# Activation stage of a hybrid decoder layer: how its one-hots, gate tiles and gate stores are formed

## The reference

```python
q = (xb @ wq).reshape(PEER_BLOCK, PEER_HEADS, 2, PEER_HALF)
s = jnp.einsum('thpd,hpkd->thpk', q, subkeys).astype(jnp.float32)
s_top, i_top = lax.top_k(s, PEER_TOPK)
cand = s_top[:, :, 0, :, None] + s_top[:, :, 1, None, :]           # 256 pairs a head
g_s, g_i = lax.top_k(cand, PEER_TOPK)
e = jnp.take_along_axis(cand_idx, g_i, axis=-1)                    # expert = i * 128 + j
g = jax.nn.softmax(g_s, axis=-1)
act = jax.nn.gelu(jnp.einsum('thed,td->the', u[e], xb))
return jnp.einsum('the,thed->td', g * act, v[e])
```

## Time and profile before

| | |
|---|---|
| median of 3 runs | 2477.82 us (2477.76 to 2481.19) |
| the profiled execution | 2477.28 us, span 2475.5 us |
| PE busy | 2105.6 us, 85% |
| DVE busy | 1687.7 us, 68% |
| POOL busy | 929.6 us, 38% |
| ACT busy | 812.3 us, 33% |
| moved by DMA | 547.71 MB, 220 GB/s of HBM traffic over the span |
| u columns, PE line 2374 | 3072 matmuls |
| one-hots, PE line 2390 | 768 records, eight to a unit |

### The profile page before, as it was taken

One profiled execution on the slowest core, in us unless ns is written; L12 is line 12 of the kernel. 1 busy time (PEld: TensorE's weight loads), 2 busy tenths in 40 slices (PEclk: granted clock), 3 DMA queues, 4 the chain that ended last, 5 costly groups with the idle time before them and its releaser, 6 DMA issues. The chain is left out here.

```text
span 2475.5 us, 31968 instructions
## 1 busy us (share of the span) xinstructions
PE 2105.6 (85%) x10417; PEld 1698.3 (69%) x10417; DVE 1687.7 (68%) x3076; ACT 812.3 (33%) x1519; POOL 929.6 (38%) x727
## 2 busy tenths in 40 slices
PE   8998976678887867969888788888877899999997
PEld 7774763334334646858788788887777788888885
DVE  4562007867231134798999999998756899998988
ACT  1331012133101021123455455455454333333331
POOL 1000333222000000015666556666666556554550
PEclk9999997687989688989899889989988899999998
DMA  5323429765513102226677777777878999999993
GB/s 188 78 53 109 141 84 317 285 233 207 201 61 109 51 0 80 64 84 220 199 258 249 230 234 258 252 251 241 292 261 315 373 397 392 395 397 392 387 386 126
DMA packets 243183, 547.71 MB, mean 221 GB/s; under 512 B 21598, under 2 KB 125712, under 8 KB 241771
## 3 DMA queue, kind: packets, MB, share of 16 engines
q1 hardware_dynamic: 114538, 287.33, 33.7%
q0 software_dynamic: 60736, 208.40, 23.0%
q10 hardware_dynamic: 67776, 50.34, 6.3%
HBM read 485.51 MB, written 60.02 MB: 220 GB/s over the span
## 5 line engine op out<-in xcount | busy, mean ns | idle before, releaser
L2374 PE MATMUL psum<-hH,uH 128*128 128x384 f32 x1024 | 364.8, 356 | 58.9 <-PEq L1934 19.7
L2076 POOL DMA_INDIRECT u_gather<-in_u_rows,gather_ids x160 | 202.5, 1266 | 520.0 <-DVE gather_ids L1889 421.9
L2192 POOL TENSOR_TENSOR uL<-u_raw,uH 128x1024 fp32r<-128x1024 f32 x125 | 312.4, 2500 | 197.6 <-ACT uH L2206 196.2
L2374 PE MATMUL psum<-hL,uH 128*128 128x384 f32 x1024 | 354.6, 346 | 0.0
L2374 PE MATMUL psum<-hH,uL 128*128 128x384 f32 x1024 | 353.9, 346 | 0.0
L2482 POOL DMA_INDIRECT v_gather<-in_v_rows,idx_now x160 | 252.7, 1579 | 235.4 <-DVE y_sample L2567 139.1
L2270 DVE CUSTOM_DVE_ANT_0 u_prod<-u_gather,h 128x1024 f32<-128x1024 f32 x160 | 251.5, 1572 | 102.8 <-DMA u_gather<-in_u_rows,gather_ids 94.8
L2616 PE MATMUL psum<-vH,wH 128*128 128x512 f32 x768 | 301.7, 393 | 21.3 <-DVE wL L2560 21.3
L2616 PE MATMUL psum<-vH,wL 128*128 128x512 f32 x768 | 301.1, 392 | 0.0
L2616 PE MATMUL psum<-vL,wH 128*128 128x512 f32 x768 | 300.7, 392 | 0.0
L2374 PEld LDWEIGHTS psum<-hH,uH 128*128 128x128 f32 x1024 | 202.8, 198 | 63.9 <-issue 42.8
(11 more groups left out here) (482 smaller groups left out, 3518.8 us busy)
## 6 DMA issues: line engine op xcount, KB each, us to landing
u_raw<-in_uT SPq DMA_DIRECT2D x128, 512.0 KB, 4.5
S<-in_v_rows SPq DMA_DIRECT2D x64, 512.0 KB, 10.6
v_rest<-in_v_rows SPq DMA_DIRECT2D x64, 512.0 KB, 6.7
activation_table<-acts ACTq DMA_DIRECT2D x128, 192.0 KB, 4.3
gate_table<-Gtile ACTq DMA_DIRECT2D x12, 2048.0 KB, 15.6
S<-gate_table SPq DMA_DIRECT2D x16, 768.0 KB, 7.8
S<-activation_table SPq DMA_DIRECT2D x16, 768.0 KB, 11.4
G_rest<-gate_table SPq DMA_DIRECT2D x16, 768.0 KB, 7.4
```

What stands on the lines that cost most here:

```text
L2076: c.nc.gpsimd.indirect_dma_start(c.ug[:, k % RG], None, c.A["u_rows"].rearrange("j i d -> (j i) d"), bass.IndirectOffsetOnAxis(ap=c.ids[:, ...
L2192: nc.gpsimd.tensor_tensor(uL[:, n % RU], u[:, n % RAW], uH[:, n % RU].bitcast(F32), ALU.subtract).then_inc(u_split, 1)
L2374: ins = nc.tensor.matmul(bank[n % 2][:, 0:ND], w[:, n % RU, d], x[:, d], start=m == 0, stop=m == len(parts) - 1)
```

## The change

In `stage_activate` the two one-hot tiles become one, `hot[:, buffer, 0:8]`, with i in 0 to 3 and j in 4 to 7. DVE makes the first six in one operation. ACT makes the last two: |j - iota|, then Relu(gate - gate x distance), which is the gate where they are equal and 0 elsewhere; the other two j are scaled as before. So ACT runs six operations of 128 elements a unit. PE writes token t's tile to every fourth column of the bank, and the eviction then reads the bank in order. The unit's order on ACT is evict, then a quarter of a gate store, then gate. A finished block is stored as four transfers, one in each of the next four units. `acts` has three buffers. Pass 0 has eight dots instead of twelve, the last pass 52 instead of 48. In the expert stage the five sums of the first group come behind its products and first three splits; in other groups the order is as it was. The route buffer of the sample is smaller.

```diff
-STEP_DOTS = ((2, 1) * 4, (6, 5) * 4, (6,) * 8, (6,) * 8)
+STEP_DOTS = ((1,) * 8, (6, 5) * 4, (6,) * 8, (7, 6) * 4)
...
+RA = 3
+BY_DVE = UNIT // 2
+STORES = 4
...
                 def slots_in(p):
                     act.wait_ge(res_mm, p)
-                    nc.scalar.activation(slots[:],
-                                         bank[5][:, 0:3 * P].rearrange("p (q n) -> p q n", q=3),
+                    nc.scalar.activation(slot_g[:, 0], bank[5][:, 2 * P:3 * P], ACT.Copy)
+                    nc.scalar.activation(slot_g[:, 1], bank[5][:, 2 * P:3 * P], ACT.Copy, scale=-1.0)
+                    nc.scalar.activation(slot_ij[:].rearrange("p u q t -> p q u t"),
+                                         bank[5][:, 0:2 * P].rearrange("p (q u t) -> p q u t", q=2, t=UNIT),
                                          ACT.Copy).then_inc(slots_ready, 1)
...
-                    nc.scalar.activation(G[:, blk % 2, :, j * UNIT:(j + 1) * UNIT].rearrange("p j t -> p t j"),
-                                         bank[2 + n % RB].rearrange("p (t j) -> p t j", t=UNIT),
+                    nc.scalar.activation(G[:, blk % 2, :, j * UNIT:(j + 1) * UNIT],
+                                         bank[2 + n % RB].rearrange("p (j t) -> p j t", t=UNIT),
                                          ACT.Copy).then_inc(g_ev, 1)
...
+                def store(blk, i):
+                    if i == 0:
+                        act.wait_ge(g_ev, (blk + 1) * BUNIT)
+                    part = slice(i * (NG // STORES), (i + 1) * (NG // STORES))
+                    act.dma_start(A["gates"][part, :, blk * (GS * TB):(blk + 1) * (GS * TB)].rearrange("g p n -> p g n"),
+                                  G[:, blk % 2].rearrange("p (g j) t -> p g (j t)", j=GS)[:, part]
+                                  ).then_inc(G_stored[blk % 2], 16)
+
+                def gate(p, n):
+                    k, h = n % PUNIT, n % RH
+                    act.wait_ge(slots_ready, p)
+                    if n >= RH:
+                        act.wait_ge(g_mm, n - RH + 1)
+                    for q in range(BY_DVE, UNIT):
+                        ins = nc.scalar.activation(hot[:, h, UNIT + q], c.iota[:], ACT.Abs,
+                                                   bias=slot_ij[:, k, 1, q:q + 1], scale=-1.0)
+                    ins.then_inc(distance, 1)
+                    act.wait_ge(hot_ready, n + 1)
+                    for q in range(BY_DVE):
+                        nc.scalar.activation(hot[:, h, UNIT + q], hot[:, h, UNIT + q], ACT.Copy,
+                                             scale=slot_g[:, 0, k * UNIT + q:k * UNIT + q + 1])
+                    act.wait_ge(distance, n + 1)
+                    for q in range(BY_DVE, UNIT):
+                        m = k * UNIT + q
+                        ins = nc.scalar.activation(hot[:, h, UNIT + q], hot[:, h, UNIT + q], ACT.Relu,
+                                                   bias=slot_g[:, 0, m:m + 1], scale=slot_g[:, 1, m:m + 1])
+                    ins.then_inc(gated, 1)
...
                 def unit(p, st, i):
                     n = unit_of(p, st, i)
                     j = n % PUNIT
-                    act.wait_ge(slots_ready, p)
-                    for k in range(j + GATE_LEAD if j else 0, min(j + GATE_LEAD + 1, PUNIT)):
-                        act.wait_ge(hot_ready, n - j + k + 1)
-                        for q in range(UNIT):
-                            ins = nc.scalar.activation(hot_j[:, k % RH, q], hot_j[:, k % RH, q], ACT.Copy,
-                                                       scale=slots[:, 2, k * UNIT + q:k * UNIT + q + 1])
-                        ins.then_inc(gated, 1)
                     if n:
                         evict(n - 1)
+                    if n >= BUNIT and n % BUNIT < STORES:
+                        store(n // BUNIT - 1, n % BUNIT)
+                    for k in range(j + GATE_LEAD if j else 0, min(j + GATE_LEAD + 1, PUNIT)):
+                        gate(p, n - j + k)
+
+                def flush():
+                    evict(NUNIT - 1)
+                    for i in range(STORES):
+                        store(NTB - 1, i)
...
-                    for q, hot in enumerate((hot_i, hot_j)):
-                        ins = V.tensor_tensor(hot[:, n % RH], c.iota[:].unsqueeze(1).to_broadcast([P, UNIT, P]),
-                                              slots[:, q, j * UNIT:(j + 1) * UNIT].unsqueeze(2).to_broadcast([P, UNIT, P]),
-                                              ALU.is_equal)
-                    ins.then_inc(hot_ready, 1)
+                    made = UNIT + BY_DVE
+                    V.tensor_tensor(hot[:, n % RH, 0:made], c.iota[:].unsqueeze(1).to_broadcast([P, made, P]),
+                                    slot_ij[:, j].rearrange("p q t -> p (q t)")[:, 0:made].unsqueeze(2)
+                                    .to_broadcast([P, made, P]), ALU.is_equal).then_inc(hot_ready, 1)
...
-                        ins = nc.tensor.matmul(bank[2 + n % RB][:, q * P:(q + 1) * P], hot_i[:, n % RH, q],
-                                               hot_j[:, n % RH, q], start=True, stop=True)
+                        ins = nc.tensor.matmul(bank[2 + n % RB].rearrange("p (j t) -> p t j", t=UNIT)[:, q],
+                                               hot[:, n % RH, q], hot[:, n % RH, UNIT + q], start=True, stop=True)
...
+                    first = r is None and b == 0
+                    for j in range(GS):
+                        product(r, b, j)
+                        if j:
+                            split(r, b, j - 1)
+                        elif not first:
+                            split(r, b - 1, GS - 1)
+                        if j == 0:
+                            dve.wait_ge(w_taken, g + 1)
+                        if not first:
+                            add(r, b, j)
+                    for s in range(0 if first else GS, GR):
+                        add(r, b, s)
```

More of the change, by code:

```diff
@@ L1897, in __init__ @@
         self.v16, self.cand = sb("v16", [P, 2, TOPK]), sb("cand", [P, TOPK * TOPK])
-        self.first, self.second, self.sample = ((sb("i16_" + n, [P, BATCH, 2, TOPK], U32), sb("gi_" + n, [P, BATCH, TOPK], U32))
-                                                for n in ("first", "second", "sample"))
+        self.first, self.second, self.sample = ((sb("i16_" + n, [P, k, 2, TOPK], U32), sb("gi_" + n, [P, k, TOPK], U32))
+                                                for n, k in (("first", BATCH), ("second", BATCH), ("sample", 2)))
         self.ab, self.abf = sb("ab", [P, BATCH, 2, TOPK], U32), sb("abf", [P, BATCH, 2, TOPK])
@@ L2093, in stage_activate @@
         a = c.acts
-        slots, prod = sb("slots", [P, 3, P]), sb("u_prod", [P, D])
+        slot_ij, slot_g, prod = sb("slot_ij", [P, PUNIT, 2, UNIT]), sb("slot_gate", [P, 2, P]), sb("u_prod", [P, D])
         b = c.route
         gsum = sb("gsum", [P, PH])
-        hot_i, hot_j = (sb(n, [P, RH, UNIT, P]) for n in ("hot_i", "hot_j"))
+        hot = sb("hot", [P, RH, 2 * UNIT, P])
         G = sb("Gtile", [P, 2, NKEYS, TB])
@@ L2180, in _ @@
                 for i in range(2):
-                    sp.wait_ge(G_stored[i], 16 * (NTB // 2))
-                    sp.wait_ge(a_stored[i], 16 * (GS // 2))
+                    sp.wait_ge(G_stored[i], 16 * STORES * (NTB // 2))
+                for i in range(RA):
+                    sp.wait_ge(a_stored[i], 16 * len(range(i, GS, RA)))
                 sp.dma_start(c.G_group[0], A["gates"][0]).then_inc(c.G_in[0], 16)
@@ L2211, in columns @@
                     act.wait_ge(u_mm, n + 1)
-                    if n >= 2:
-                        act.wait_ge(a_stored[n % 2], 16 * (n // 2))
-                    nc.scalar.activation(a[:, n % 2], bank[n % 2][:, 0:ND], ACT.Gelu_apprx_tanh).then_inc(u_act, 1)
+                    if n >= RA:
+                        act.wait_ge(a_stored[n % RA], 16 * (n // RA))
+                    nc.scalar.activation(a[:, n % RA], bank[n % 2][:, 0:ND], ACT.Gelu_apprx_tanh).then_inc(u_act, 1)
                     act.wait_ge(u_act, n + 1)
-                    act.dma_start(A["acts"][n], a[:, n % 2]).then_inc(a_stored[n % 2], 16)
+                    act.dma_start(A["acts"][n], a[:, n % RA]).then_inc(a_stored[n % RA], 16)
                 def gates_out(p):
@@ L2449, in _ @@
                     sp.dma_start(v[j], A["v_rows"][j]).then_inc(v_in[j], 16)
-                for i in range(2):
-                    sp.wait_ge(c.a_stored[i], 16 * (NKEYS // 2))
+                for i in range(RA):
+                    sp.wait_ge(c.a_stored[i], 16 * len(range(i, NKEYS, RA)))
                 def body(r, b):
@@ L2573, in body @@
                                   ).then_inc(w_taken, 1)
-                    product(r, b, 0)
-                    if r is not None or b:
-                        split(r, b - 1, GS - 1)
-                    dve.wait_ge(w_taken, g + 1)
-                    add(r, b, 0)
-                    product(r, b, 1)
-                    split(r, b, 0)
```

(12 more changed lines are left out.)

13 lines of the change are left out of this document (4 added, 9 removed).

## The result

The changed kernel takes 2460.17 us (median, 2456.82 to 2462.97) against 2477.79 for the one before beside it: ratio 0.9927, 95% interval 0.9909 to 0.9944. Faster, but by 18 us where 93 were forecast, and outside the range. Its profiled execution has a span of 2458.0 us.

The account below looks back on a forecast made before the run. DVE and PE were taken to run neck and neck, with ACT's store stalls holding nearly all DVE slack. Stretches of 83, 214, 216 and 173 us make 686 against 773 (-87), experts -6: 2477.3 - 93 = 2384 us, range 2353 to 2442.

Parts of the forecast that it names:

- the stall term: Activation passes: removing ACT's store stalls gives DVE 4.5 us each, 13.5 us for three in a pass; PE 25 us.
- Pass 3: Last activation pass: falls from 196 us to PE's floor of 173 us, with DVE below 138 and ACT 147.
- Pass 0: Activation stage's first stretch: four dots fewer save DVE 7.7 us before the first routing, 91 us becoming 83.
- One-hot term: DVE in each pass: one merged one-hot operation saves 10.9 us, and less waiting for GpSimd's subtractions saves 4 us.
- ACT's cost: ACT's cycle per unit: 3.95 us becomes 4.98 with six gating operations and store issues, 4.6 after eviction's gain; PE's is 5.06.
- Rival A: Strided PSUM writes double the unit's 0.81 us of one-hot matmuls, giving back 54 us, 2438 us; chance 0.17.
- Rival B: Four quarter stores block ACT's queue as long as one whole, 10.2 us a block; about +30 us, 2414 us; chance 0.07.
- Rival C: Abs not in gelu's table, so each unit swaps ACT tables twice; cycle 7.5 us, total 2531 us; chance 0.04.
- Rival D: DVE's waiting for GpSimd halves, passes fall to PE's floors, 23 us less, 2361 us; chance 0.70 jointly with the forecast.
- Experts: Expert stage's start: first sums moved behind splits start PE 6.2 us sooner, at 1919.3, and this carries to the end.
- The tail: Activation stage from 1880 us: no change counted, since its last gate store still goes out at once.

Follow-up runs that it names:

- e1: Kernel before with only the gate stores changed: each block stored in four quarters over the next four units; 2478.26 us, ratio 1.0001.
- e6: e4 with each gate block stored as one whole 2 MB transfer instead of quarters; 2442.26 us, ratio 0.9848.
- e4: Changed kernel with four dots put back from the last pass to pass 0 (twelve there, 48 in pass 3); 2434.12 us, ratio 0.9817.
- e11: e4 with the last gate block's four quarter stores spread, one in each of the first four tail columns; 2430.8 us, ratio 0.9811.
- e3: Changed kernel with GpSimd's subtraction cut to 128 of 1024 elements, all waits kept; 2349.97 us, ratio 0.9491.
- e13b: e4 with the last pass's 48 dots in steps of seven and five instead of six; 2446.89 us, ratio 0.9868.
- e7: e4 with all eight one-hots of a unit in one DVE operation, none on ACT; 2456.43 us, ratio 0.9909.
- e12: e4 with gate tiles unbroken in PSUM as before the change, the eviction going across them; 2439.76 us, ratio 0.9842.
- e2: Kernel before with GpSimd's subtraction cut to 128 of 1024 elements, all waits kept; 2361.14 us, ratio 0.9526.
- e15b: e11 with the expert stage's first-group sums back in the order of the kernel before; 2432.97 us, ratio 0.9810.

## Why the prediction was wrong, step by step

**The step that failed is the stall term, 13.5 us in pass 1 and again in pass 2.** The prediction took 4.5 us of DVE's idle time in each stall as slack that it would fill with work once the stall is gone, at the same collision rate. Both halves were wrong. The size came from one window with 5.5 us of idle time; 40 us that lie in the same way round the other two stalls of that pass have 3.7 and 3.6 (before):

```profile
1294.00:1334.00 40.00, 33.49 (x193) 33.04 (x192) 36.26 (x68) 22.04 (x44) 26.63 (x16) 0.91 0.77 254
1354.00:1394.00 40.00, 33.55 (x201) 33.10 (x200) 36.45 (x65) 19.45 (x39) 26.37 (x16) 0.91 0.80 265
```

All of DVE's waits that the profile lists in that pass are for gathered rows:

```profile
DVE u_prod L2270 <- DMA u_gather<-in_u_rows,gather_ids: 12.5, 6, 2.9
```

Only one of them, of 2.2 us, lies inside a stall; three come some 10 us behind one. e1, with the stalls alone taken out, idles 7.7 and 7.1 us less in passes 1 and 2, not 13.5, and DVE's busy time rises by 5.2 and 7.0: it gained nothing. e6 put the stalls back into the new kernel and lost nothing in these two passes. And the kernel after, without stalls, still leaves DVE idle for 17.6 us of pass 1 and 13.8 of pass 2, by the same cuts, where before left 19.5 and 17.4: the slack was not the stalls' alone.

DVE is the bound there, and a quarter of its busy time is collisions. My account of the rise is this: while ACT stands still, GpSimd, which waits for ACT's uH, stands soon too, and DVE works that time off uncontended. The trace of before fits: GpSimd subtracts during 24% of its nine stalls in the passes and during 41% of the rest, and the dots begun in a stall take 1314 ns against 1595. Kind by kind against the means outside, the DVE operations begun in the nine stalls are 12.5 us shorter in all (an estimate from these means); e1's DVE is busy 11.4 us longer than before's over the three passes. That this is the whole coupling stays my reading; no run isolates it. In pass 3, where DVE has room, the stalls do cost PE: 14 us by e6 (e1: 6.5), under the 25 forecast for three, and the tail takes part of it back (4 us in e6, 6.8 in e1).

**Pass 3, forecast 173 (PE's floor).** The floor was near enough: 176 in e4, 174 in e11, 170 in e3. The kernel had 199, since "four dots move to the last pass, where DVE has 58 us to spare" counted busy time and not order. Two thirds of the 23 us come from having seven dots in a step, one third from the four dots more (e13b, after).

**Pass 0, forecast -7.7.** Nothing came that the spread of the kernels lets me see. DVE did lose 6.9 busy us there, but its first routing then waited 14.4 us for ACT's exponential where it had waited 4.1, and ACT stands behind PE and PE behind GpSimd's subtractions, whose queue waits for dots. Why it waited longer stays open; no run tried it. The waits of 1107 to 1198 us, after and then before:

```profile
POOL u_gather L2079 <- DVE dots L2301: 22.0, 3, 11.8
...
DVE gsum L2316 <- ACT res_first L2224: 14.4, 1, 14.4
```
```profile
DVE gsum L2285 <- ACT res_first L2220: 4.1, 1, 4.1
```

e4 and the other kernels with twelve dots say that the four dots were nearly free in pass 0.

**One-hot term, -10.9 and -4 a pass.** Right: the earlier trace rows and the groups after give 89.0 + 64.1 + 5.5 against 55.0 + 75.1 + 14.1, 14.4 us less in pass 1. The collisions did not go with the operations, they moved to the dots and the routing, as the prediction chose. Passes 1 and 2 are by 15 and 12 us shorter, most of it this term: DVE's busy time fell by 13.1 and 8.6 between the copies of the slots. e7 gives two of eight on ACT 17.6 us over three passes.

**ACT's cost.** 0.60 + six operations of which the Relu takes 480: the cycle stays under PE's, and ACT is busy 63% in pass 3 (forecast 60).

**Rival A, strided PSUM writes: refuted.** In the trace after a unit's eight records span 1.05 us as in the earlier trace rows, and e12, which takes the stride away, is not faster. The rule of the Trainium skill ("Advanced Engine Details and Errata", section "PSUM Cachelines"), that a non-contiguous pattern significantly slows matmuls, did not show for 128-column f32 matmuls whose results lie 16 bytes apart:

```profile
1330.11 1.05 PE L2420 MATMUL psum<-hot 128*128 128x128 f32 x8
```

**Rival B, the stall splits: not in the passes**, where every store of an activation takes 0.34 to 0.36 us; but four quarters in one row do hold ACT (14.26 us). Its price had a slip: it gives ACT 159 us in pass 3 where the sum has 147 (32 x 4.6), and with 147 it is 15 us, not 30. **Rival C, table swaps: refuted**, the stage's gelu line has six loads, as before:

```profile
L2218 ACT ACT_TABLE_LOAD x6 | 7.7, 1283 | 0.1
```

**Rival D, collisions halve: no.** e2 shows what lay there: with the long subtraction gone, 4.7% or some 117 us.

**Experts, -6.2.** The start came as forecast: 1902.64 is 7.6 us behind the last dot's start, before 14.0. It is given back. The time from the last dot to the span's end is 561.4 to 564.0 us in the four kernels with the old order (before, e1, e2, e15b) and 559.3 to 564.0 in the others. The trace says where: after 200 matmuls of the stage PE is 62.5 us behind the last dot's start in the kernel after and 62.3 in the one before, and from there both keep one pace. Two waits for a low part lie between that before does not have, and with the second PE's granted clock falls (0.77 over the stretch shown):

```profile
1918.00 0.50 PE L2644 MATMUL psum<-vH,wH 128*128 128x512 f32 x1 [1.17 <-DVE wL L2590]
...
1937.89 0.80 PE L2644 MATMUL psum<-vH,wH 128*128 128x512 f32 x1 [3.26 <-DVE wL L2590]
```
```profile
1930.00:1945.00 15.00, 11.74 (x40) 9.19 (x39) 10.69 (x14) 4.60 (x6) 5.36 (x5) 0.77 1.03 406
```

The first is the fourth weight. The prediction had it ready 11.6 us behind PE's start; it came after 15.3, since three of the five sums ahead of it waited for gathered rows (0.47, 0.63 and 1.27 us), which the prediction put at nothing. The second is the eighth. Its low part stands behind DVE's first product of the third group, and that waits for its activation tile, here after and then before:

```profile
1935.68 0.56 DVE L2579 TENSOR_TENSOR wf<-S 128x384 f32<-128x384 f32 x1 [3.06 <-DMA S<-activation_table]
```
```profile
1954.45 0.56 DVE L2549 TENSOR_TENSOR wf<-S 128x384 f32<-128x384 f32 x1 [2.19 <-DMA S<-activation_table]
```

Counted from the last dot it comes 40.7 us behind it after and 42.9 before: 2.2 us sooner, where PE began 6.4 sooner. So at that place PE waits for what the transfers bring. DMA's share of 1.03 in that stretch points at the transfers' rate; no run took transfers away, so this last step stays argued.

**The tail, forecast 0.** It is 6 us longer by the earlier trace rows's cut. The step took the last gate store as going out at once, but it goes as four. From the last eviction to the last dot, with eight dots in the tail, the kernels with whole stores have 31.3 and 31.2 us (before, e6; e2, without collisions, 23.7), those with four quarters in one row 34.5 to 38.4 (e3 33.3), e1 among them with 38.1, and those with the quarters spread 33.4 to 35.0. So the growth goes with splitting the stores, and ACT's hold of 14 us is at most a part of it (under 1 us by e11 against e4). By what way the rest comes is open.

**The sum.** By the cuts of the earlier trace rows the forecast lost 8 us in pass 0, 36 in passes 1 and 2 (27 of them the stall term), 21 in pass 3, 6 in the tail and 5 in the experts: 76, and 93 less 76 is the 18 measured, within 1 us. The table's finer cuts give 30 us lost in passes 1 and 2 (27 of them the stall term) and 26 in pass 3. By the ratios the change is worth 45 us with the dots left in pass 0 (e4), and 47 with the tail's stores spread as well (e11, 2430.8 us, faster than both kernels).

## What to carry to other kernels

Before pricing idle time of a bound engine as slack, add the idle time up over all such places, and ask what the busy time is made of: here a quarter was collisions with GpSimd, and taking the stalls away turned idle time into longer operations. When a few operations move to a stage with spare time, look at where in the in-order list they land and what stands behind them; a step of seven dots cost 15 us at the same number. Cutting the disputed work to an eighth, with all waits left in place, told in one run what no row of the profile did, though it shortens GpSimd's own work as well. And work that starts sooner gains nothing when its inputs arrive as before.

## What the runs showed of the hardware

- Beside a GpSimd subtraction of 128 x 1024 DVE's one-hot operation of 768 elements takes 3.16 us at worst instead of 0.94. With the subtraction cut to an eighth the kernel is 4.7% shorter, some 117 us (e2).

```profile
L2329 DVE TENSOR_TENSOR hot<-iota,slot_ij x96: 943/952/3160, 1199.4 to 1844.0; 128x768 f32<-128x768 f32 x96
```

- A gate store of 2 MB takes 0.39 us to issue and then holds the next store of the same queue about 10 us. Behind quarters of 512 KB one unit apart the next store takes 0.34 to 0.36; four in one row hold it 14.26 us, four some 5 us apart 0.39 to 1.33 each (e11).
- Relu with a scale and a bias from SBUF takes 480 ns on 128 x 128, Copy with a scale 392, Abs with a bias 393. An eviction of 128 x 512 that writes across 128-byte strides takes 1082 to 1132 ns, one that writes 16-byte runs 596.
